# The lengths of queries and keys in a gated DeltaNet branch: taken for each token and head in a column, or spread over all partitions by a ones matrix

## The reference

```python
def l2_normalize(x):
    return x * lax.rsqrt(jnp.sum(jnp.square(x), axis=-1, keepdims=True) + RMS_EPS)

q = l2_normalize(heads(q)) * (GDN_HEAD_DIM ** -0.5)
k = l2_normalize(heads(k))
...
kk = jnp.where(strict, jnp.einsum('bhnid,bhnjd->bhnij', k_beta, k) * decay, 0.0)
qk = jnp.einsum('bhnid,bhnjd->bhnij', q, k) * decay
```

## Time and profile before

| | us |
|---|---|
| median of 3 runs | 1323.68 |
| lowest and highest | 1322.41, 1324.08 |
| the profiled execution | 1322.69 |
| its span in the trace | 1320.9 |
| TensorE busy in the span | 1244.5 |
| VectorE busy | 429.7 |
| ScalarE busy | 243.7 |
| POOL busy | 146.8 |

### The profile page before, as it was taken

How to read it: one execution, slowest core, us unless ns; L and a number is a source line. 1 busy time by engine, 2 the same in 40 slices (tenths; PEclk the granted TensorE clock), 3 DMA queues, 4 the chain that set the end, 5 groups by cost and what they waited for, 6 DMA issues and landing times.

```text
span 1320.9 us, 16687 instructions
## 1 busy us (share of the span) xinstructions
PE 1244.5 (94%) x6851; PEld 636.9 (48%) x6851; DVE 429.7 (33%) x795; ACT 243.7 (18%) x399; POOL 146.8 (11%) x103
## 2 busy tenths in 40 slices
PE   5888999999898999999999999999999999989996
PEld 5788899899883333333333333333333233333332
DVE  5486564145562212222122221222121122221224
ACT  4444335344431000000000000000000000000001
POOL 6222442245510000000000000000000000000000
PEclk9898999999889999999999999999999999999998
DMA  9432322176578999999999999999999999999995
GB/s 312 151 110 104 128 90 103 64 276 234 172 302 352 428 427 427 427 428 428 427 429 427 427 427 428 428 428 428 428 427 428 428 427 429 428 426 427 426 426 217
DMA packets 56982, 453.35 MB, mean 343 GB/s; under 512 B 7453, under 2 KB 11626, under 8 KB 32362
## 3 DMA queue, kind: packets, MB, share of 16 engines
q1 hardware_dynamic: 56938, 452.71, 83.0%
HBM read 451.64 MB, written 1.05 MB: 343 GB/s over the span
## 4 chain that ended last, share of the span: by engine, by line
PE 67%; DMA 21%; DVE 7%; issue 2%; ACT 2%; SPq 1%; POOL 0%; DVEq 0%
PE bank L1297 23%; DMA late<-in_w_gate_up_dram 17%; PE bank L1369 14%; PE bank L1121 5%; PE bank L1122 4%; PE bank L1123 4%; PE bank L1382 3%; DMA raw<-in_w_gate_up_dram 3%; PE bank L1268 3%; DVE early L1547 2%; PE bank L1283 2%; PE bank L1357 1%; ACT late L1093 1%; PE bank L541 1%; PE bank L546 1%
## 5 line engine op out<-in xcount | busy, mean ns | idle before, releaser
L1297 PE MATMUL bank<-late 128*64 128x512 f32 x1424 | 321.4, 595 | 12.5 <-DMA late<-in_w_gate_up_dram 12.5
L1297 PEld LDWEIGHTS bank<-late 128*64 128x64 f32 x1424 | 96.9, 136 | 213.1 <-issue 184.7
L1369 PE MATMUL bank<-late 128*64 128x512 f32 x704 | 159.4, 604 | 3.7 <-ACT late L1093 3.7
L1297 PE MATMUL bank<-raw,late 128*64 128x512 f32 x624 | 140.7, 596 | 2.4 <-DMA raw<-in_w_gate_up_dram 2.4
L725 POOL TENSOR_TENSOR w_lo<-raw,w_hi 128x1024 fp32r<-128x1024 f32 x47 | 114.6, 2441 | 223.0 <-ACT w_hi L994 223.0
L1121 PE MATMUL bank<-act_hi,w_hi 128*128 128x256 f32 x448 | 130.5, 291 | 5.0 <-DVE w_lo L725 4.0
L1122 PE MATMUL bank<-act_lo,w_hi 128*128 128x256 f32 x448 | 127.3, 284 | 0.0
L1123 PE MATMUL bank<-act_hi,w_lo 128*128 128x256 f32 x448 | 127.2, 284 | 0.0
L1701 DVE TENSOR_SCALAR late<-bank 128x512 f32<-128x512 f32 x32 | 22.1, 692 | 317.7 <-PE bank L1297 317.6
L994 ACT CAST w_hi<-raw 128x1024 fp32r<-128x1024 f32 x84 | 87.6, 1044 | 121.0 <-issue 74.6
L1369 PEld LDWEIGHTS bank<-late 128*64 128x64 f32 x704 | 49.2, 138 | 99.8 <-issue 90.5
(11 more groups left out here) (317 smaller groups left out, 1227.5 us busy)
## 6 DMA issues: line engine op xcount, KB each, us to landing
late<-in_w_gate_up_dram SPq DMA_DIRECT2D x89, 2048.0 KB, 36.5
late<-in_w_down_dram SPq DMA_DIRECT2D x44, 2048.0 KB, 36.3
raw<-in_w_gate_up_dram SPq DMA_DIRECT2D x39, 2048.0 KB, 34.6
raw<-in_w_down_dram SPq DMA_DIRECT2D x20, 2048.0 KB, 38.2
raw<-in_w_in_dram SPq DMA_DIRECT2D x14, 2048.0 KB, 7.7
raw<-in_w_br_dram SPq DMA_DIRECT2D x3, 2048.0 KB, 7.7
raw<-in_w_o_dram SPq DMA_DIRECT2D x2, 2048.0 KB, 8.8
raw<-in_w_mem_kv_dram SPq DMA_DIRECT2D x4, 512.0 KB, 7.4
```

The lines of the kernel that those rows point to most:

```text
L1297: ins = mm(bk[64 * c:64 * c + 64, :], x_slotT[:, k % 4, 64 * (k // 4):64 * (k // 4) + 64], w[:, kk, at + 512 * c:at + 512 * (c + 1)], star ...
L1369: ins = mm(ps[3][64 * c:64 * c + 64, :], hidT[:, kk, 64 * q:64 * q + 64], w[:, kk, c * 512:(c + 1) * 512], start=(q == 0 and kk == 0), sto ...
```

## The change

The ones matrix (128x128) becomes the weights and the squares the moving side, 512 columns at a time. Each of four products fills one of the banks 4 to 7 with the sum over the 128 partitions, already on every partition. ScalarE takes the roots of the four banks in place, and VectorE the reciprocals of the four banks in place, one after the other, before its four products with the banks. The second pass of TensorE ("lengths") and `inv_norm` are gone; VectorE's part of "norms" no longer waits for ScalarE.

```diff
--- before.py
+++ after.py
@@ -240,7 +240,6 @@
         chunk_decay = tiny.new(NPB, 2)
         s_max, s_neg, s_sum, s_rec = (tiny.new(H, NT) for _ in range(4))
         o_ss, o_rs = tiny.new(NPB), tiny.new(NPB)
-        inv_norm = tiny.new(NT, 2 * H)
 
 
 
@@ -421,7 +420,7 @@
         GP, GD, GA = {}, {}, {}
         gp = gd = ga = 0
         for name in GDN_STEPS:
-            gp += name != "olen"
+            gp += name not in ("olen", "lengths")
             GP[name] = gp
             ga += {"lx0": 0, "decay": 3, "norms": 1, "tokens": 1, "kcum": 1, "olen": 1}.get(name, 1 if name.startswith(("lx", "state")) else 0)
             GA[name] = ga
@@ -442,8 +441,9 @@
                 a.activation(decayT, decayT, ACT.Exp).then_inc(g_act, 1)
             elif name == "norms":
                 act.wait_ge(g_pe, GP["norms"])
-                a.activation(inv_norm.rearrange("p t h -> p (t h)"), ps[4][:, 0:2 * NPB], ACT.Sqrt,
-                             bias=eps_rms[:, 0:1]).then_inc(g_act, 1)
+                for n in range(4):
+                    ins = a.activation(ps[4 + n][:, :], ps[4 + n][:, :], ACT.Sqrt, bias=eps_rms[:, 0:1])
+                ins.then_inc(g_act, 1)
             elif name == "tokens":
 
                 act.wait_ge(g_pe, GP["tokens"])
@@ -506,17 +506,11 @@
                 pe.wait_ge(g_dve_sq, 1)
                 pe.wait_ge(g_dve, GD["decay"])
                 pe.wait_ge(g_act, GA["decay"])
-                for t in range(NT):
-                    for n in range(2 * H):
-                        ins = mm(ps[4][:, t * 2 * H + n:t * 2 * H + n + 1], squares[:, n, t * P:(t + 1) * P], ones[:, 0:1],
-                                 start=True, stop=True)
+
+                for n in range(4):
+                    ins = mm(ps[4 + n][:, :], ones[:], squares[:, 2 * n:2 * n + 2, :], start=True, stop=True)
             elif name == "lengths":
-
-                pe.wait_ge(g_dve, GD["norms"])
-                for n in range(2 * H):
-                    for t in range(NT):
-                        ins = mm(ps[4 + n // 2][:, (n % 2) * T + t * P:(n % 2) * T + (t + 1) * P],
-                                 spread(inv_norm, t, n), ident[:], start=True, stop=True)
+                return
             elif name == "scores":
                 pe.wait_ge(g_dve, GD["lengths"])
                 for p in range(NPB):
@@ -613,11 +607,12 @@
 
                 v.wait_ge(g_act, GA["decay"])
                 step(d.tensor_tensor(bexp, bexp, beta, ALU.mult))
-                step(d.tensor_copy(chunk_decay, expg[:, :, CHUNK - 1::CHUNK]))
-                v.wait_ge(g_act, GA[name])
-                d.reciprocal(inv_norm, inv_norm).then_inc(g_dve, 1)
+                d.tensor_copy(chunk_decay, expg[:, :, CHUNK - 1::CHUNK]).then_inc(g_dve, 1)
             elif name == "lengths":
-                v.wait_ge(g_pe, GP[name])
+                v.wait_ge(g_dve, GD["norms"])
+                v.wait_ge(g_act, GA["norms"])
+                for n in range(4):
+                    step(d.reciprocal(ps[4 + n][:, :], ps[4 + n][:, :]))
                 for n in range(2):
                     o = flat(kT)[:, 512 * n:512 * n + 512]
                     d.tensor_tensor(o, o, ps[6 + n][:, :], ALU.mult)
```

## The result

The changed kernel took 1330.93 us (median of 6 runs, 1330.02 to 1334.86) against 1323.58 us of the kernel before (6 runs, 1322.41 to 1324.13): 7.3 us more, a ratio of 1.0063 with a 95% interval of 1.0052 to 1.0074. Its profiled execution took 1331.12 us with a span of 1329.4 us. In the changed kernel the lines after the edit have moved up by a few; L511 are the four sums, L615 the reciprocals, L618 and L621 the products with the banks, L517 and L519 "scores".

What follows compares the result with a forecast made beforehand. The prediction took the experts' weight stream on DMA, started by the mixer, as the bound. "Scores" 3.3 us late plus 1.7 us of clock gave 5.0 us, added to 1323.68 us for 1328.7 us; range 1325 to 1334.5 us.

Steps and rivals of the forecast that it cites:

- the shift at 145 us is not the shift at the end: Sign of a wrong prediction: a delay around 145 us, after "scores", that differs from the delay at the kernel's end.
- What bounds the kernel, and that a shift passes whole to the end: Whole kernel: the experts' weight stream fills the DMA, so a shift of the mixer moves the end by as much.
- Rival (c): End of the kernel: the delay is real but the DMA stream catches up; 1323.7 us, chance 0.06.
- TensorE's sums, 5.2 us with 3.3 us of low clock: Four products in "norms": 5.2 us in all, 3.3 us of it at low clock, ending at 116.4 us.
- ScalarE, 2.2 us: ScalarE's four roots of 128x512 in the banks: 2.2 us, from 116.6 us to 118.8 us.
- The reciprocal, 3.43 us: VectorE's wide reciprocals ahead of the products with the lengths: 3.43 us each, bounds 3.30 and 4.22 us.
- Rival (a): VectorE's wide reciprocals: slow at 8.0 ns a column, 4.22 us each; 1331.9 us, chance 0.30.
- The 4.4 us that the prediction's signs name: Sign in the profile after: four reciprocals of 128x512 at 3.3 to 4.4 us each.
- Rival (b): VectorE's wide reciprocals: ordinary price, 0.65 us each, so 7.0 us are saved; 1316.7 us, chance 0.05.
- "Scores" 3.3 us late and 1.7 us of clock, 5.0 in all: TensorE at "scores": starts 3.3 us late behind VectorE, then loses 1.7 us to low clock after idling.
- rival (d): TensorE's clock stays high in "norms" and "scores" loses nothing: 1.7 us late, 1325.4 us, chance 0.08.
- From 'scores' on the order is that of before, moved as a whole: Everything behind "scores": same order, moved as a whole, with nothing added to the 5.0 us.

Runs made afterwards that it cites:

- the second profile: Profile of the changed kernel run once more with no edit; median 1330.83 us, ratio 1.0053 to the kernel before.
- the kernel with the constant: Changed kernel with the four wide reciprocals replaced by multiply-adds that write 0.09 to the banks, leaving out the lengths; median 1316.24 us, ratio 0.9945.
- the one kept busy: Changed kernel with ten products of 128x512 into an unread bank ahead of TensorE's wait for "scores"; median 1326.46 us, ratio 1.0021.
- the wide reciprocals in the kernel before: Kernel before with only the reciprocals moved into the four banks, the narrow one becoming a copy; median 1337.86 us, ratio 1.0099.
- four more reciprocals: Changed kernel with two banks inverted three times in place of once, same result; median 1343.46 us, ratio 1.0151.
- the delay of 12: Kernel before with 12 idle multiplications of 128x512 on VectorE ahead of its products with the lengths; median 1326.77 us, ratio 1.0025.
- its filler: Kernel before with three products of 128x512 into an unread bank in TensorE's gap ahead of "norms"; median 1321.17 us, ratio 0.9981.
- the delays of 8 and 17: Kernel before with 8 or 17 idle multiplications on VectorE ahead of its products with the lengths; medians 1322.3 us and 1333.99 us.
- the logarithm: Changed kernel with ScalarE's logarithm and exponential in the banks in place of root and reciprocal; median 1317.71 us, ratio 0.9953.

## Why the prediction was right

The time lies in the range (1325 to 1334.5 us), on the side that was forecast, 2.2 us above the 1328.7 us named. The step that it rests on, the price of the wide reciprocals and TensorE's wait for them, is shown. But one of its own signs of being wrong came true: the shift at 145 us is not the shift at the end. The split on POOL is 3.3 us late in the first profile (145.83 against 142.49 us) and 5.5 us in the second (148.01), the end 8.4 and 8.1 us. A part of the loss has a source that the sum left out, and it was luck that the range, made wide for other unknowns, had room for it. By its steps:

- **What bounds the kernel, and that a shift passes whole to the end:** held, by the table. Rival (c) is out. That the end is late by nothing else did not hold (last point).
- **TensorE's sums, 5.2 us with 3.3 us of low clock:** 5.26 us in the second profile and 5.4 us in four experiments, but 3.70 us, all at full clock, in the first. The term is one of chance, and the bounds were right to have both. The sum rests on the 0.111 us of a record at 1.00 and on the share of full speed that the trace gives for the clock, not on GHz. At one column a clock, an estimate, the 1.2 GHz that the prediction writes beside 0.50 agree with z3 of the kernel before, where 256 columns came every 0.213 us at 0.50, and its 2.4 GHz are twice that; in xc0 and xc1 256 columns came every 0.120 us at 1.00.
- **ScalarE, 2.2 us:** 2.39 us; that is 0.2 us over the row of the copy, with the writes to the banks in it.
- **The reciprocal, 3.43 us:** 3.37 us. The row pair of 8 and 16 columns named the slope (6.4 ns, measured 6.3); the other pairs in hand, at 6.1 and 8.0 ns, would have given 3.30 and 4.22 us. The narrow ones lie in SBUF and the wide ones in a bank, and no run takes a wide one in SBUF, so the 6.3 ns hold what the bank adds. Rival (a) with 4.22 us is out. The 4.4 us that the prediction's signs name as the upper end of a reciprocal are shown by no row and no run: the rows reach to 4.22 us, and the 24 wide ones in five profiles took 3.37 us each. Rival (b), the ordinary price, is out as well; the kernel with the constant shows that its time was right (1316.7 named, 1316.24 measured).
- **"Scores" 3.3 us late and 1.7 us of clock, 5.0 in all:** in the second profile it started at 135.74 us, 3.8 us late or 3.2 with the 0.58 us of its later start taken off, and its end was 5.0 us late by the same count. In the first profile the short sums made it 3.8 us. The wait was 10.0 and 10.1 us, 10.3 named. Of rival (d) the first profile has one half, the sums at full clock, but not the other: "scores" ran at half clock behind the wait in both.
- **"From 'scores' on the order is that of before, moved as a whole":** this is the term that was sized wrongly. The order did stay, but it was priced at nothing, and in the profiles of the changed kernel the clock withheld 1.7 and 5.2 us more behind "scores" (10.2 and 13.7 against 8.5 us). The loss of the medians is 7.3 us where 5.0 were added up; the missing 2.3 us lie between these two, while the terms of the sum, measured together at the edit, came to 3.8 and 5.0 us. The prediction looked for the clock only where the change makes a gap; behind short gaps that both kernels have, near 154 and 400 us, it can fall too. TensorE idles 1.93 us ahead of the first of these places and 1.58 us ahead of the second in the first profiles of both kernels, and the clock fell there in the changed one (0.51) and not in the one before (1.00).

What stays open: why the stretch after the first products of the solve came in both profiles of the changed kernel, in the one kept busy, with the wide reciprocals in the kernel before, with four more reciprocals and with the delay of 12, but in neither profile of the kernel before, nor with its filler, with the delays of 8 and 17, with the constant or with the logarithm. It needs neither the ones matrix nor the reciprocals, and a later "scores" is not enough for it. With one profile of most kernels, chance is not ruled out for a single one.

## What to carry to other kernels

Take a reciprocal on VectorE on as few columns as possible, before a broadcast and not behind it: a wide one took 3.37 us here where a multiply-add of the same bank took 0.70 us, nearly five times as much. Narrow durations in the trace of before are enough to tell that it is dear; three pairs of them put it at 3.30 to 4.22 us. The ones-matrix form pays once root and reciprocal are taken by ScalarE (6.0 us here; 7.6 us with a cheap operation in place of the reciprocal). When a change shifts TensorE's work, count its short gaps behind the edit with a few microseconds of clock either way, and profile twice before a difference of that size is explained.

## What was not expected of the hardware

- A float reciprocal of 128x512 costs 3.37 us on VectorE where a multiply-add of the same bank costs 0.70 us.
- TensorE's clock fell in one-column products with no gap ahead of them: 1.00 for the first 2.1 us, then 0.50, with TensorE busy throughout by its records. Products of 512 columns in the same place, behind the same filler, kept 3.70 us and the full clock (1.00 from 111.0 to 114.7 us). Each is one execution.
- The multiplication of 128x512 by a constant within SBUF took 0.46 us, less than the 0.65 us of a product of two operands, one of them in a bank. In the execution with 17 of them one took 2.62 us while POOL's split ran, the other 16 took 0.44 us each; it is one case, and its cause was not tested.
- ScalarE loaded a table of 1.28 us between the logarithm and the exponential.
